# One transformer-like layer pair on Trainium2: token shift and mixes moved into the projection program, and reordered work around the output matrix and the feed-forward

## What is computed

```python
def rwkv7_mixer(z, mu, w0, w2, a0, a2, g2, k_k, k_a, r_k, gn_g, gn_b):
    bsz, t, _ = z.shape
    z = z + (token_shift(z) - z) * mu
...
def hybrid_mixer(h, w_in, ...):
    proj = h @ w_in
...
    merged = (gates[:, :, 0] * (y_a @ sc_out) + gates[:, :, 1] * (y_b @ sb_out)
              + gates[:, :, 2] * (y_c @ rw_out) + gates[:, :, 3] * (y_d @ sg_out))
    return merged @ w_o

def conv_glu_ffn(h, w_up, conv_w, w_down):
    up = causal_dwconv(h @ w_up, conv_w)
    gate, val = jnp.split(up, 2, axis=-1)
    return (jax.nn.silu(gate) * val) @ w_down
```

## Time and profile before

| | |
|---|---|
| median of three runs | 1651.3 us |
| the profiled execution: time, span | 1651.11 us, 1649.3 us |
| PE, DVE, ScalarE, GpSimd busy | 1587.9, 1180.9, 827.8, 435.5 us |
| mean granted TensorE clock | 0.987 of full |
| weights and others read | 270.65 MB |

### The profile page before, as it was taken

The page is one execution under the profiler, slowest core; times in us unless marked ns, Lnnn a source line. Parts: engine busy times, 40 slices in busy tenths (PEclk is TensorE's granted clock), DMA queues, the critical chain, the costliest instruction groups (busy, mean ns, idle before and its releaser), DMA issues. The chain is left out here.

```text
span 1649.3 us, 34054 instructions
## 1 busy us (share of the span) xinstructions
PE 1587.9 (96%) x11842; PEld 1462.3 (89%) x11842; DVE 1180.9 (72%) x2295; ACT 827.8 (50%) x1357; POOL 435.5 (26%) x261
## 2 busy tenths in 40 slices
PE   7997999999998999999999999999999999999997
PEld 7987987999998977789999999999999888888886
DVE  5666326687786877716699996777774777777776
ACT  5364334455554463233556454555555555555554
POOL 1245540044441003456668990000000000000000
PEclk9988999999999999999999999999999999999999
DMA  8522444356663421155558775655557777777763
GB/s 288 158 62 82 127 142 128 128 180 183 186 215 118 167 77 52 59 176 197 157 170 234 217 221 165 176 177 176 182 177 223 245 241 240 232 237 238 239 227 123
DMA packets 92812, 289.56 MB, mean 176 GB/s; under 512 B 10304, under 2 KB 27072, under 8 KB 92352
## 3 DMA queue, kind: packets, MB, share of 16 engines
q1 hardware_dynamic: 92304, 287.61, 55.3%
q10 hardware_dynamic: 432, 0.90, 0.2%
HBM read 270.65 MB, written 17.83 MB: 175 GB/s over the span
## 5 line engine op out<-in xcount | busy, mean ns | idle before, releaser
L265 PE MATMUL psum<-arena_parts,ring_parts 128*128 128x256 f32 (+1 forms) x1856 | 525.2, 283 | 0.0
L263 PE MATMUL psum<-arena_parts 128*128 128x256 f32 (+2 forms) x1664 | 479.4, 288 | 26.5 <-DVE ring_parts L258 11.7
L2756 DVE TENSOR_TENSOR ring_parts<-ring,arena_parts 128x512 fp32r<-128x512 f32 x418 | 282.7, 690 | 112.8 <-ACT arena_parts L2550 94.8
L265 PEld LDWEIGHTS psum<-arena_parts,ring_parts 128*128 128x128 f32 x1856 | 356.0, 192 | 0.0
L263 PEld LDWEIGHTS psum<-arena_parts 128*128 128x128 f32 x1664 | 316.3, 190 | 29.5 <-DVE ring_parts L258 10.7
L264 PE MATMUL psum<-h_parts,arena_parts 128*128 128x256 f32 x1024 | 287.1, 280 | 0.0
L258 POOL TENSOR_TENSOR ring_parts<-ring,arena_parts 128x1024 fp32r<-128x1024 f32 x79 | 209.7, 2677 | 67.7 <-ACT arena_parts L254 48.8
L2519 PE MATMUL psum<-arena_parts,x_parts 128*128 128x512 f32 x512 | 201.4, 393 | 0.8 <-DVE x_parts L2783 0.8
L2520 PE MATMUL psum<-ring_parts,x_parts 128*128 128x512 f32 x512 | 201.7, 394 | 0.0
L2521 PE MATMUL psum<-arena_parts,x_parts 128*128 128x512 f32 x512 | 201.4, 393 | 0.0
L264 PEld LDWEIGHTS psum<-h_parts,arena_parts 128*128 128x128 f32 x1024 | 194.4, 190 | 0.0
(11 more groups left out here) (547 smaller groups left out, 3270.3 us busy)
## 6 DMA issues: line engine op xcount, KB each, us to landing
ring<-stream SPq DMA_DIRECT2D x473, 512.0 KB, 3.7
kept<-arena SPq DMA_DIRECT2D x128, 128.0 KB, 2.0
arena<-kept SPq DMA_DIRECT2D x32, 512.0 KB, 4.5
arena<-first SPq DMA_DIRECT2D x1, 2144.0 KB, 16.7
arena<-second SPq DMA_DIRECT2D x1, 1632.0 KB, 6.6
x<-x_t SPq DMA_DIRECT2D x1, 1024.0 KB, 5.5
out<-arena SPq DMA_DIRECT2D x4, 256.0 KB, 2.1
arena<-last ACTq DMA_DIRECT2D x1, 512.0 KB, 3.4
```

The lines of the kernel that those rows point to most:

```text
L263: nc.tensor.matmul(dst, stationary[0], moving[0], start=first, stop=False)
L265: return nc.tensor.matmul(dst, stationary[1], moving[0], start=False, stop=last_one)
L2756: v.tensor_tensor(low[:, s, w], ring[:, s, w], expert_high[:, m % 2, w].bitcast(F32), ALU.subtract)\
```

## The change

Four edits. (1) DVE's token shift and the eight mixes are issued in the projection program: the subtract after the work of block 12, two mixes after each of the blocks 13 to 16. (2) In the output program, PE multiplies the first seven k tiles of output blocks 0 and 1, then the last tile of both, then the other blocks; DVE writes the remainders of blocks 0 and 1 after tiles 4 and 6. (3) In a feed-forward pass, DVE first scales and convolves and then writes all three remainders, and ScalarE does silu before the second rounding; the tail after the loop is interleaved in the same way. (4) PE's last pass is taken out of the loop and has both pairs of up blocks before the two down blocks.

```diff
@@ build, declarations
+        shift = Area(arena, scratch_at).take(8, T)
...
-        shift = a2.take(8, T)
+        a2.take(8, T)
@@ projection program, DVE, in the loop over n
+                    if n == 12:
+                        vec.link(v.tensor_tensor(shift[:, :, 1:T], z[:, 0:8, 0:T - 1], z[:, 0:8, 1:T], ALU.subtract))
+                        vec.link(v.tensor_scalar(shift[:, :, 0:1], z[:, 0:8, 0:1], -1.0, None, ALU.mult))
+                    if 13 <= n < 17:
+                        for c in (2 * n - 26, 2 * n - 25):
+                            ins = v.scalar_tensor_tensor(z[:, c, :], shift[:, c, :], col("rw_mu", c), z[:, c, :],
+                                                         ALU.mult, ALU.add)
+                        if n == 16:
+                            ins.then_inc(S("rw_mixed"), 1)
@@ mixer program, DVE
-                vec.link(v.tensor_tensor(shift[:, :, 1:T], z[:, 0:8, 0:T - 1], z[:, 0:8, 1:T], ALU.subtract))
-                vec.link(v.tensor_scalar(shift[:, :, 0:1], z[:, 0:8, 0:1], -1.0, None, ALU.mult))
-                for c in range(8):
-                    ins = v.scalar_tensor_tensor(z[:, c, :], shift[:, c, :], col("rw_mu", c), z[:, c, :],
-                                                 ALU.mult, ALU.add)
-                vec.tell(ins, S("rw_mixed"))
+                dve.wait_ge(S("rw_mixed"), 1)
@@ output program, PE
-                project(pe, W_O[:4], range(4), 1, onto(0))
-                project(pe, W_O[4:], range(4), 1, onto(4))
+                for m in range(2):
+                    onto(m, range(KT - 1))
+                for m in range(2):
+                    onto(m, range(KT - 1, KT))
+                for m in range(2, KT):
+                    onto(m, range(KT))
+                pe_at.advance(W_O, 1, None)
+                for b in range(4):
+                    pe_at.banks[b] += 2
@@ output program, DVE, in the loop over tiles
-                        if k == 6:
-                            weights_low(0)
-                weights_low(1)
+                        if k in (4, 6):
+                            weights_low(k // 2 - 2)
@@ feed-forward program, PE
-                with pe.Fori(0, pairs) as i:
+                with pe.Fori(0, pairs - 1) as i:
                     for j in range(2):
                         up(3 * j, i)
                         down(3 * j + 2, i, j)
+                for j in range(2):
+                    up(3 * j, pairs - 1)
+                for j in range(2):
+                    down(3 * j + 2, pairs - 1, j)
@@ feed-forward program, DVE
-                        ff_low(dve, 3 * j, i)
                         scale_up(i, j)
-                        ff_low(dve, 3 * j + 1, i)
                         convolve(i, j)
-                        ff_low(dve, 3 * j + 2, i)
-                for j in range(2):
-                    ff_low(dve, j, pairs)
-                for j in range(2):
-                    scale_up(pairs, j)
-                    convolve(pairs, j)
+                        for part in range(3):
+                            ff_low(dve, 3 * j + part, i)
+                scale_up(pairs, 0)
+                convolve(pairs, 0)
+                ff_low(dve, 0, pairs)
+                scale_up(pairs, 1)
+                convolve(pairs, 1)
+                ff_low(dve, 1, pairs)
@@ feed-forward program, ScalarE
                         ff_high(act, 3 * j, i)
+                        silu(i, j)
                         ff_high(act, 3 * j + 1, i)
                         ff_high(act, 3 * j + 2, i)
-                        silu(i, j)
                 for j in range(2):
                     ff_high(act, j, pairs)
-                for j in range(2):
                     silu(pairs, j)
```

26 lines of the change are left out of this document (14 added, 12 removed).

## The result

| | kernel before | with the change |
|---|---|---|
| median | 1648.8 us (1646.9 to 1653.5, 9 runs) | 1639.2 us (1638.3 to 1647.4, 9 runs) |
| profiled execution: time, span, clock | 1651.11, 1649.3 us, 0.987 | 1643.34, 1641.6 us, 0.988 |

The ratio is 0.9948, with a 95% interval of 0.9930 to 0.9965: 5.8 to 11.5 us faster. (The nine runs lie unevenly; their mean is 1641.0.) The two profiled executions differ by 7.8 us, where 6.8 had been forecast. The three times of the kernel before that stood ahead of the prediction are among the four highest of its nine here.

The account below looks back on a forecast made before the run. PE, busy for 96% of the span, was taken as the bound, so only its idle time could go. The terms 0 + 2.2 + 4.5 + 0.1 = 6.8 us, from 1651.1, gave 1644.3 us, range 1641.3 to 1648.2.

Parts of the forecast that it names:

- The base: Level the gains were subtracted from: profiled execution 1651.1 us, taken to stand alike with the median of three runs, 1651.3.
- Shift and mixes, 0: Mixer program: moving 7.3 us of DVE work gains 0, with 0.9 us as the other end.
- the turn with GpSimd: Mixer: GpSimd's subtract holds DVE's L664, which still ends at 113.4 though issued 0.9 us earlier.
- 0.9 us: Mixer: most the moved mixes can gain, as DVE's chain starts again at ScalarE's logarithm, 107.8 instead of 101.4.
- The naive 7.3: Mixer: all 7.3 us of moved DVE work saved if the logarithm did not bind either, 1637.0 us; chance 0.04.
- Output matrix, 2.2: Output program: PE waits of 0.97 and 1.40 us become one of about 0.5; gain 2.2 us.
- Feed-forward, start, 4.5: First down block: the 2.90 us wait and the 1.2 GHz time behind it go; gain 4.5 us.
- Loop, 0: Feed-forward loop: DVE takes 7.9 us per half pass, below PE's 8.46, so the loop costs nothing more.
- Feed-forward, end, 0.1: Last pass: about 0.9 us of wait stays, DVE ends 13.3 us behind; gain 0.1, between -1.5 and 1.2.
- Rival 2, the clock: Behind the feed-forward, changed spacing spares PE a stretch at 1.2 GHz worth 1.4 us: 1642.9 us; chance 0.08.
- Rivals 3 and 4: Start wait moves to up block 1 or 4, costing 1.5 to 4 us (0.17); the loop's circle binds, 1659 us (0.06).
- rivals 1 and 2: Mixes give 0.9 us, 1643.4 (0.12), or all 7.3, 1637.0 (0.04); spared 1.2 GHz stretch behind feed-forward, 1642.9 (0.08).

Follow-up runs that it names:

- the repetition: The whole change run once more beside new runs of the kernel before, on another chip: 1641.0 us (9 runs), ratio 0.9951.
- the unrolled pass alone: Kernel before with only PE's last feed-forward pass taken out of the loop and reordered: 1649.0 us (10 runs), ratio 1.0017.
- the last kernel: Whole change plus both edits of DVE's mixer program (min operations before logarithm wait, TensorE's next rows first) and GpSimd's second short convolution earlier: 1633.5 us, ratio 0.9907.
- the order alone: Kernel before with only the order of DVE and ScalarE in the feed-forward changed: 1645.8 us (10 runs), ratio 0.9989.
- the earlier logarithm edit: Whole change, with DVE's three min operations put ahead of the wait for ScalarE's logarithm: 1640.4 us (6 runs), ratio 0.9946.
- the last two kernels: Whole change with both edits of DVE's mixer program, 1637.3 us, ratio 0.9926; the same with GpSimd's second short convolution moved earlier, 1633.5 us, ratio 0.9907.

## Why the prediction was wrong, and where it was right

- **The base, the step that failed.** "The profiled execution took 1651.1 us ... and the median of three runs is 1651.3, so they stand alike": they agreed because both were high draws. 87 runs of the kernel before have a median of 1648.7, and 23 of them lie at 1650.6 or above. The range took in the uncertainty of the terms and none of the base. 1648.7 - 6.8 would have been 1641.9, inside the stated range. Of the 5.1 us between forecast and median the base is 2.4 and the terms are about 1.1 (7.9 instead of 6.8). The remaining 1.6 are the draw of nine runs; the repetition's median was 1641.0.
- **Shift and mixes, 0:** the mechanism is right (the logarithm, then the turn with GpSimd; both shown). The bound was wrong: "**0.9 us**, no more" was the distance of DVE from the logarithm in one profile, and the six profiles with the old place had 1.0 to 4.6. The size is likely 1 to 1.5 us and not shown. The naive 7.3 is excluded.
- **Output matrix, 2.2:** 2.3. The wait left over was 0.31 instead of 0.5.
- **Feed-forward, start, 4.5:** from the first matmul PE runs without a pause at full clock. PE took 192.5 us from the first to the last matmul (317.91 to 510.39) and now 187.5 (315.39 to 502.91). Of these 5.0 us 0.5 belong to the end (1.19 to 0.71), so 4.5. The wait of 2.9 us was read rightly. That the number came out is in part luck: 1.4 of it is the time at 1.2 GHz behind the wait, which two of the four profiles with the wait did not have.
- **Loop, 0:** right. DVE is busy 142.8 us of the stretch that had 135.0, and nothing waits: the circle stays under 8.46 us.
- **Feed-forward, end, 0.1:** 0.9 (0.5 in the wait for GpSimd, 0.4 in DVE's end). DVE's end (503.23) stood 12.3 us behind that of the last up block (490.9: PE's end less four blocks and the wait) instead of the 13.3 taken, inside the stated 11 to 15.4. Beside that of the mixes this is the term that was mis-sized.
- **Rival 2, the clock:** the profiles show no effect of the change either way. In this pair PE spent more time at 1.2 GHz behind the feed-forward with the change: 6.82 us from the same first matmul hold 42 matmuls before and 33 after, below. PE had idled 0.71 and 2.91 us ahead of it, before 1.19 and 3.29. But the second profile of the whole change has 42 matmuls and a granted clock of 0.75 there, just as the kernel before, and other profiles lie between 0.55 (the unrolled pass alone) and 1.00 (the last kernel).

```profile
513.68:520.50 6.82, 6.82 (x42) 6.82 (x43) 5.72 (x11) 4.30 (x8) 0.00 (x0) 0.75 0.59 229
```
```profile
505.83:512.65 6.82, 6.82 (x33) 6.82 (x34) 5.72 (x11) 4.30 (x8) 0.00 (x0) 0.57 0.47 198
```

Rivals 3 and 4 did not occur: no wait of an up block, no loop stall. The range's lower end was meant to hold rivals 1 and 2; what took the median below it was mostly the base and not one of them.

## What to carry over

Taking work off a queue pays only up to the next thing the queue waits for; look behind the removed rows for the first operation with a releaser of its own. Ask also for whom a late value is made and what stands ahead of it: in the profile, moving what TensorE wanted next to the front took 6.8 us from the stretch, and removing 7.3 us of other work a fraction of that. When a change is worth less than the spread of the runs, the base deserves a term and an interval like any other: three runs and one profile at a clock of 0.987 were some 2.5 us above the level. And a distance or a spell of lower clock read from one profile is one draw too: the 0.9 us and the 1.4 us here both were.

## What had not been expected of the hardware

- The price of a turn falls unevenly. GpSimd's remainder lasts 2.4 us with or without VectorE beside it when it is there first, and VectorE's 0.69 us operations then last up to 2.85. The other way round GpSimd waits, but for less. In the last kernel, where the subtract had begun at 107.07 and ended at 109.25, GpSimd's remainder shows 3.00 us, which is 2.4 from 109.1:

```profile
108.50 3.00 POOL L353 TENSOR_TENSOR ring_parts<-ring,rounded 128x1024 fp32r<-128x1024 f32 x1 [0.87 <-ACT rounded L254]
```

  That fits what the Trainium skill ("SBUF — State Buffer", "Who interferes with whom") says on who blocks: by it the one that issues first keeps the shared pair for its whole instruction. The prediction had used the rule on the subtract alone; in the mixer of the change four rows of VectorE further on (L689, L691, L697, L698) are stretched in the same way, to 2.59, 5.05 (two operations), 2.72 and 2.71 us.
- A small VectorE operation (128x2) can also be held, 1.52 us instead of 0.17.
- The same wait need not cost the same clock: after 2.90 and 2.87 us of idle PE was granted 0.66 in the next 4.23 us, after 2.75 and 2.74 it was granted 1.00.
- The second layer's last part, which no edit touched, ran at two rates at the same granted clock: 434 to 435 matmuls per 100 us in eight of the fourteen profiles (the kernel before and both of the whole change among them), 430 to 431 in six (the shift alone, the order alone, both feed-forward parts, the earlier logarithm edit, and the last two kernels). The rows below are the kernel before and the shift alone. From the second layer's first matmul to the end these two took 1135.6 and 1139.3 us, of which some 1.2 are the clock right behind the barrier (0.75 and 0.58 over 6.82 us, an estimate). What is left is as large as the parts measured, and its cause stays open.

```profile
1300.00:1400.00 100.00, 100.00 (x435) 81.29 (x433) 74.21 (x145) 56.76 (x109) 0.00 (x0) 1.00 0.72 237
```
```profile
1300.00:1400.00 100.00, 100.00 (x430) 80.37 (x430) 73.72 (x144) 55.86 (x108) 0.00 (x0) 1.00 0.71 236
```
